# Four moves in a two-layer hybrid kernel: the last state-space outputs, the D scaling, one chunk of GpSimd's weighting, two slices of a down projection

## What is computed

```
xs, bm, cm = jnp.split(xbc, [SSM_D_INNER, SSM_D_INNER + SSM_GROUPS * SSM_STATE], axis=-1)
for d in range(2):
    v_ssm = (xs * dt[..., None]).reshape(b, L, SSM_GROUPS, SSM_RATIO, SSM_HEADDIM)
    y, s = chunked_decay_scan(fl(cm), fl(bm), fl(v_ssm), fl(la_ssm), s0)
    ssm_ys.append(fl(y).reshape(b, L, SSM_HEADS, SSM_HEADDIM) + d_skip[d][:, None] * xs)
y_ssm = (ssm_ys[0] + ssm_ys[1]).reshape(b, L, SSM_D_INNER)
y_ssm = rms_norm(y_ssm * jax.nn.silu(z)) * norm_gain
```

```
def conv_ffn(h, w_up, conv_w, conv_b, w_down):
    u = dwconv3(h @ w_up, conv_w, conv_b)
    a, val = jnp.split(u, 2, axis=-1)
    return (jax.nn.silu(a) * val) @ w_down
```

## Time and profile before

| | us |
|---|---|
| median of 3 runs | 1973.29 |
| lowest and highest | 1973.1, 1974.2 |
| the profiled execution's own time | 1970.14 |
| its span in the trace | 1968.4 |
| PE busy (share of the span) | 1896.4 (96%) |
| DVE busy | 1267.4 (64%) |
| ACT busy | 817.2 (42%) |
| POOL busy | 122.5 (6%) |

### The profile page before, as it was taken

How to read it: one execution, slowest core, us unless ns; L and a number is a source line. 1 busy time by engine, 2 the same in 40 slices (tenths; PEclk the granted TensorE clock), 3 DMA queues, 4 the chain that set the end, 5 groups by cost and what they waited for, 6 DMA issues and landing times.

```text
span 1968.4 us, 33247 instructions
## 1 busy us (share of the span) xinstructions
PE 1896.4 (96%) x13415; PEld 1800.2 (91%) x13415; DVE 1267.4 (64%) x2101; ACT 817.2 (42%) x1367; POOL 122.5 (6%) x106
## 2 busy tenths in 40 slices
PE   7999999999999999999999999899999999999999
PEld 4998789999988899999999989866698999999999
DVE  5555944666877877878978876656536553553553
ACT  4645732222435355234234344555525541441441
POOL 0011200000010000000000025411100000000000
PEclk9999999999999999999999999999999999999999
DMA  8221012444321323443433322100012222222222
GB/s 308 86 77 34 17 49 89 140 147 151 102 81 54 129 100 119 144 128 115 152 128 115 110 89 68 57 1 1 1 54 61 74 69 80 76 71 76 75 69 79
DMA packets 57065, 175.96 MB, mean 89 GB/s; under 512 B 7552, under 2 KB 9472, under 8 KB 56832
## 3 DMA queue, kind: packets, MB, share of 16 engines
q1 hardware_dynamic: 55152, 172.17, 27.1%
q10 hardware_dynamic: 1808, 2.36, 0.3%
HBM read 170.05 MB, written 4.46 MB: 89 GB/s over the span
## 4 chain that ended last, share of the span: by engine, by line
PE 84%; DVE 9%; ACT 4%; issue 2%; DMA 1%; SPq 1%; POOL 0%; ACTq 0%; DVEq 0%
PE ps L379 70%; PE ps L2103 2%; PE ps L2088 2%; DVE t_sb L772 1%; DVE h_lo L782 1%; PE ps L879 1%; DVE w_lo L368 1%; PE ps L2056 1%; DVE PT L2220 1%; PE ps L1294 1%; PE ps L2055 1%; ACT w_hi L360 1%; PE ps L1281 1%; PE ps L1305 1%; DMA x<-in_x 1%
## 5 line engine op out<-in xcount | busy, mean ns | idle before, releaser
L379 PE MATMUL ps<-h_hi,w_hi 128*128 128x320 f32 x2768 | 637.5, 311 | 7.8 <-DVE w_lo L368 2.9
L379 PE MATMUL ps<-h_lo,w_hi 128*128 128x320 f32 x2768 | 633.0, 310 | 9.0 <-DVE h_lo L782 7.8
L379 PE MATMUL ps<-h_hi,w_lo 128*128 128x320 f32 x2768 | 629.8, 308 | 0.0
L368 DVE TENSOR_TENSOR w_lo<-raw,w_hi 128x1024 fp32r<-128x1024 f32 (+1 forms) x218 | 267.2, 1226 | 452.6 <-ACT w_hi L360 452.3
L360 ACT ACTIVATE w_hi<-raw 128x1024 fp32r<-128x1024 f32 (+1 forms) x221 | 230.6, 1043 | 695.4 <-PE ps L379 695.2
L379 PEld LDWEIGHTS ps<-h_lo,w_hi 128*128 128x128 f32 x2768 | 461.4, 188 | 16.1 <-DVE h_lo L782 14.5
L379 PEld LDWEIGHTS ps<-h_hi,w_hi 128*128 128x128 f32 x2768 | 460.5, 188 | 15.1 <-issue 5.2
L379 PEld LDWEIGHTS ps<-h_hi,w_lo 128*128 128x128 f32 x2768 | 462.6, 188 | 0.0
L379 PE MATMUL ps<-hid_hi,w_hi 128*128 128x320 f32 x704 | 160.9, 309 | 4.4 <-DVE hid_lo L981 2.5
L379 PE MATMUL ps<-hid_hi,w_lo 128*128 128x320 f32 x704 | 160.2, 308 | 0.0
L379 PE MATMUL ps<-hid_lo,w_hi 128*128 128x320 f32 x704 | 160.2, 308 | 0.0
(11 more groups left out here) (285 smaller groups left out, 2014.7 us busy)
## 6 DMA issues: line engine op xcount, KB each, us to landing
raw<-in_ffn_up SPq DMA_DIRECT2D x88, 512.0 KB, 3.6
raw<-in_hyb_in SPq DMA_DIRECT2D x49, 512.0 KB, 3.8
mrawB<-in_w_modB SPq DMA_DIRECT2D x48, 512.0 KB, 4.2
mrawA<-in_w_modB SPq DMA_DIRECT2D x64, 256.0 KB, 2.8
raw<-in_ffn_down SPq DMA_DIRECT2D x32, 448.0 KB, 3.3
raw<-in_hyb_out SPq DMA_DIRECT2D x16, 512.0 KB, 4.2
raw<-in_ffn_down SPq DMA_DIRECT2D x16, 512.0 KB, 3.6
modw<-in_w_modA SPq DMA_DIRECT2D x12, 512.0 KB, 13.3
```

Source lines behind the costliest of these rows:

```text
L368: eng.tensor_tensor(w_lo[:, i % 2, 0:n], raw[:, b % RAW, 0:n], w_hi[:, i % 2, 0:n].bitcast(F32), SUB).then_inc(S("w_lo"), 1)
L379: last = pe.matmul(pj(f)[:, hh, :], w[:, i % 2, k * 128:(k + 1) * 128], v[:, k, hh * HALF:(hh + 1) * HALF], start=(k == 0 and n == 0), sto ...
```

## The change

There are four edits.

1. In `pe_ssd` the last iteration no longer issues the outputs of pass 7. `pe_z` writes its first unit out slice by slice and issues them, all five chunks, between the slices 4 and 5 of that unit.
2. In `act_ssd` the D scaling stands behind the copy of the final state, ahead of the exponentials of load 3; before it stood between the exponentials of loads 1 and 2.
3. In `pool_ssd` the weighting for direction 0 covers chunks 0 to 3, and no longer chunk 4.
4. In `pe_first` the three down stages of layer 0 take four slices of unit 1 ahead of the last slice of unit 0, and no longer two. Layer 1 keeps two.

```diff
-                steps = [(0, k) for k in range(K - 1)] + [(1, 0), (1, 1), (0, K - 1)] + [(1, k) for k in range(2, K)]
+                m = 4 if units[0][0].name[:3] == "dn0" else 2
+                steps = [(0, k) for k in range(K - 1)] + [(1, k) for k in range(m)] + [(0, K - 1)] + [(1, k) for k in range(m, K)]
...
-                if p:
+                if 0 < p < PAIRS:
                     pe_out(pe, p - 1, (0, 1, 2))
...
-                if p:
+                if 0 < p < PAIRS:
                     pe_out(pe, p - 1, (3, 4))
...
                         act_decay(act, p, i)
-                        if i == 1:
-                            act_skip(act, p)
                     act.wait_ge(S("ssd_kv"), p + 1)
...
                                    ACT.Copy).then_inc(S("ssd_so"), 1)
+                    act_skip(act, p)
                     act_decay(act, p, 3)
...
                 for d in range(2):
-                    scaled(xw[:, p % 2, d, :, :], wdt[:, :, d, 2 * p:2 * p + 2].unsqueeze(3).to_broadcast([128, NCH, 2, 64]))
+                    n = NCH - 1 + d
+                    scaled(xw[:, p % 2, d, 0:n, :], wdt[:, 0:n, d, 2 * p:2 * p + 2].unsqueeze(3).to_broadcast([128, n, 2, 64]), n)
...
-            for r in range(8):
-                pe_unit(pe, stages["z"], r, 0, H)
+            s = stages["z"]
+            pe_begin(pe, s, 0)
+            for k in range(KT):
+                if k == 5:
+                    pe_out(pe, PAIRS - 1, (0, 1, 2))
+                    pe_out(pe, PAIRS - 1, (3, 4))
+                last = pe_tile(pe, s, 0, k, s.u0, s.f0, H)
+            last.then_inc(S("pe_unit"), 1)
+            for r in range(1, 8):
+                pe_unit(pe, s, r, 0, H)
```

More of the change, by code:

```diff
@@ L1421, in pool_ssd, with scaled @@
                 xh = xs_chunks(p).rearrange("p c (h v) -> p c h v", h=2)
-                def scaled(out, by):
-                    pool.tensor_tensor(out.rearrange("p c (h v) -> p c h v", h=2), xh, by, MUL).then_inc(S("ssd_v"), 1)
+                def scaled(out, by, n):
+                    pool.tensor_tensor(out.rearrange("p c (h v) -> p c h v", h=2), xh[:, 0:n, :, :], by, MUL).then_inc(S("ssd_v"), 1)
                 if p >= 2:
```

## The result

| | before | changed kernel |
|---|---|---|
| median of the runs, us | 1974.2 (5 runs) | 1964.82 (5 runs) |
| lowest and highest | 1973.1, 1974.83 | 1963.59, 1964.95 |
| the profiled execution's own time | 1970.14 | 1964.69 |
| its span | 1968.4 | 1962.9 |

The ratio is 0.995, with a 95% interval of 0.9937 to 0.9964: the kernel became faster by 9.4 us. I had forecast 1966.9 and at the best 1964.9, so the direction was right and the time lies just outside the range. The table already shows what has to be explained. The two profiled executions differ by 5.45 us, less than the 6.4 of my sum. The two medians differ by 9.4.

The account below looks back on a forecast made before the run. PE was taken to bound the kernel, busy 1896.4 of 1968.4 us, with gaps and slow-clock stretches to win. Terms 4.9 + 0.9 + 0.6 + 0 = 6.4 us off the median 1973.29 gave 1966.9, range 1964.9 to 1969.9.

Parts of the forecast that it names:

- the range: Whole kernel: 8 in 10 for 1964.9 to 1969.9 us, the forecast's bounds plus some 0.6 scatter of medians either side.
- my sum: Whole kernel: the four edits' gains, 4.9 + 0.9 + 0.6 + 0 = 6.4 us; this forecast had chance 0.62.
- the gain by z's end: End of z: everything behind it is released by PE or loaded ahead, so the 5.5 us gained by then stays.
- The step that failed: Whole kernel: the 6.4 us found on the profiled execution of 1970.14 was taken off the median of 1973.29, giving 1966.9.
- Edit 1: End of passes: PE's idle 3.80 us goes and the outputs run at full clock; 4.9 us less, bounds 4.2 and 5.2.
- Edit 2: Pass 0: exponentials of load 2 and the state's copy come 0.8 earlier; 0.9 us less, bounds 0.5 and 1.1.
- the clock of pass 0 stays up too: Rival, pass 0: with the second idle stretch gone PE may stay at 2.4 GHz; gain 7.0, 1966.3 us, chance 0.10.
- Edit 3: Passes 2 to 4: shorter GpSimd instruction delays DVE less, 0.2 us three times; 0.6 us less, bounds 0 and 0.75.
- Edit 4: Layer 0 down stages: dn01 wins 0.7 us, dn02 0, dn00 loses 0.7; together 0, bounds 0.7 either way.
- a fall lands elsewhere: Clock: a fall's place differs from run to run, so the pass 0 clock rival and the forecast would both occur.

Follow-up runs that it names:

- skip_only: Kernel before with only the D scaling moved behind the final state's copy: 1971.54 us, ratio 0.9987.
- mix: fill_after with D scaling moved back, four slices only in dn01, 6 unread matmuls added in pass 0, 9 in dn02: 1963.86 us, ratio 0.9951.
- fill_after: Changed kernel plus matmuls nobody reads in PE's waits, 14 in pass 0 and 12 ahead of dn02's unit 2: 1963.89 us, ratio 0.9952.
- rest_no_z: Changed kernel with the outputs of pass 7 taken back out of z's first unit: 1968.77 us, ratio 0.9972.
- fill_before: Kernel before, order kept, plus matmuls nobody reads in four PE waits (two in pass 0, last outputs, dn01): 1968.72 us, ratio 0.9973.

## Why the prediction was off

**The sum was nearly right for the profile it was made on.** At the places of the edits matched matmuls give 7.0 (6.80 up to z's second unit and 0.16 in the down stages), against 6.4. That 1970.14 - 6.4 = 1963.7 also comes within 1.0 of the changed kernel's profiled execution, 1964.69, is luck in part: 3.1 lost in retention and 0.99 at the start stand against some 2.8 won in attention, all outside the edits. One slip in the working: it calls the gain by z's end 5.5, and its own terms are 4.9 + 0.9 + 0.6 = 6.4 there. The forecast used the 6.4.

**The step that failed is the one behind the sum**: "The median of the runs shown is 3.15 above it; the sum off the median". It takes what one profile shows for what the median gains, with the falls of the clock where that profile had them: a gain by the clock at z, where it had one, and nothing by it in pass 0, dn01 and dn02. The runs show that this doesn't hold. The same program lost 7.9 us and 12.9 us to the lower clock in two executions, filling four waits won 5.2 us on an unchanged path, and edits 2 to 4 won 5.5 (3.0 to 7.9) where the sum has 1.5.

As a sum, the 9.38 are 5.45 between the two profiled executions, plus 1974.2 - 1970.14 = 4.06 from the profile of before to its median, less 0.13 from the profile of the changed kernel to its own. I had 6.4 for the first and nothing for the difference of the other two, which is 3.9. But this 3.9 is not the edits' own: chance in retention, in attention and at the start is in it. By place, in the means of the traces, I come to an estimate of 7.4: 5.05 at z, 1.5 from pass 0 to the outputs of pass 2, 0.44 for edit 3 in passes 3 and 4, 0.16 on the path of the down stages, and by the clock 1.0 won in dn01 and 0.8 lost in dn02. That is 1.0 more than the forecast. The other 2.0 of the 9.4 stay open; the result's own interval is 7.1 to 12.4 us, so part of them can be scatter.

- **Edit 1 was right**: 5.05 in the trace against 4.9, 5.1 alone in the ratio. The outputs begin behind the fifth slice without a wait for DVE (idle 0.19 of PE's weight loads, none of its matmuls), took 2.33 at a clock of 1.00 (2.26 forecast), and the wait for `w_lo` is 0.18 (0.3 forecast). Some 1.5 of the 5.05 is the clock: it is the term of z in the table, in all six traces that kept the unfilled idle time and in none of the six with the outputs inside z.
- **Edit 2: the mechanism holds only where the clock falls, and the size was too small.** I took it for 0.9 on the path. From the first decay load to the outputs of pass 2 it is 37.06 to 38.61 us, in the mean 37.8, in the five traces with the old order unfilled, against 35.89 to 37.11, in the mean 36.3, in the five with the new order: 1.5 won, which lies in the interval of the run alone (1.0 to 4.3). Most of this is there at an equal loss in pass 0, 1.6 in the profile of before and 1.7 in `skip_only` (the first decay load and the outputs of pass 2, first before, then `skip_only`):

```profile
174.88 0.50 PE L1250 MATMUL ps<-neg_r,ident_r 128*128 128x512 f32 x1 [0.46 <-ACT t_sb L845]
212.10 0.29 PE L1305 MATMUL ps<-u_sb,xsy 128*64 128x128 f32 x1 [1.43 <-issue]
...
176.90 0.50 PE L1250 MATMUL ps<-neg_r,ident_r 128*128 128x512 f32 x1 [0.46 <-ACT t_sb L845]
212.92 0.29 PE L1305 MATMUL ps<-u_sb,xsy 128*64 128x128 f32 x1 [1.43 <-issue]
```

  That is 37.22 against 36.02, 1.2 less. PE at the lower clock is what holds the chain there: in `skip_only` DVE's pair is through 14.95 us behind the first decay load, and PE gets to the outputs of pass 0 only at 15.52 (16.72 before). So the 0.8 by which load 4 comes earlier arrives in full, and a part of the fall now lies ahead of load 4. Where the clock stays up, GpSimd meets DVE's pair, and the same move costs 0.6 (`mix` against `fill_after`). The loss in pass 0 is 1.5 to 3.1, in the mean 2.4, in the old order and 0 to 3.1, in the mean 1.6, in the new one. That the move makes the fall shorter is not shown by so few traces. My rival "the clock of pass 0 stays up too" came out once in five (`rest_no_z`), and there the stretch of 36.34 is no shorter than with a fall.
- **Edit 3 was right in mechanism**: GpSimd's pair takes 2.72 instead of 2.93 beside DVE, and PE's wait ahead of the outputs of passes 2 to 4 fell from 1.43 to 1.21, three times 0.22, 0.66 against 0.6. Alone it can't be measured in the time.
- **Edit 4 was right on the path and left out the clock.** By matched matmuls of the two traces dn00 lost 0.60, dn01 won 0.76 and dn02 is unchanged (forecast: 0.7, 0.7 and 0). But the wait of 2.50 in dn01 was followed by a fall in three of five traces, and the two waits of 0.73 in none of seven. The 2.06 in dn02 was followed by one in two of four, the 1.71 in none of seven. With 1.6 for a fall that is some 1.0 won in dn01 and 0.8 lost in dn02.
- **The range** took the scatter of medians as 0.6. Single runs of the kernel before lie between 1967.75 and 1978.14. A range drawn from one profile should have held at least a fall or two, 1.6 us each, on either side. The measured 1964.82 missed its lower end by 0.1.

The Trainium skill (TensorE: Matmul & The Clock Gate, "What's actually happening") says that the monitor of activity runs free of the kernel's start, and gives this as the reason why the point at which the clock changes varies from run to run. By that rule equal waits would be followed by a fall in some executions only, and the traces agree: three of five behind the 2.50 of dn01. My reading of it in the prediction, that a fall lands elsewhere, goes further than the traces: behind the first decay load all but one of the falls (at 1210 in `fill_before`) stand in the six places of the table.

## What to carry to other kernels

An idle time of PE costs more than its length where the clock falls behind it: list the long idle times (here a fall came behind 2.06 us and more, not behind 1.71), and shorter ones close together, and count for each a part of a fall as well, and try a few matmuls that nobody reads in them before reordering anything, since here they brought 5.2 us in an unchanged order. Take the falls out of a profile before you compare or extrapolate it, or compare the same instructions of both traces place by place, and never carry the distance between a profile and a median over to another kernel. Work moved behind a copy to free one engine stands ahead of something else: look at what the next two instructions of that engine feed.

## What the runs showed of the hardware

- **The clock falls behind waits much shorter than I had thought to matter**, and behind some of them only in a part of the executions: behind 3.80 us in six of six traces, behind 2.34 with a second one of 0.91 to 1.21 after it in five of five, behind 2.34 with at most 0.38 after it in four of five, behind 2.50 in three of five, behind 2.06 in two of four, behind 1.71 in none of seven and behind a pair of 0.73 in dn01 in none of seven. One fall costs 1.4 to 1.7 us of PE's work.
- **A long stretch at the lower clock in retention** costs 4.8 to 5.1 us in nine of the thirteen traces. In the changed kernel PE is idle 0.41, 0.50 and then 1.06 us between 557 and 562, and the clock is low until 572 although PE is busy from 562 on:

```profile
557.85 1.38 PE L1620 MATMUL ps<-qkT 64*128 64x128 f32 x10 [0.41 <-DVE x L895]
560.14 0.49 PE L1653 MATMUL ps<-vTM,PTr 128*128 128x128 f32 x2 [0.50 <-DVE PTr L1772]
561.69 0.58 PE L1653 MATMUL ps<-vTM,PTr 128*128 128x128 f32 x1 [1.06 <-DVE Sr L1762]
```

The same place as stretches of 1 us, for PE alone (length, busy time, granted clock, DMA share, GB/s):

```profile
562.00:563.00 1.00, 1.00 (x6) 0.50 0.00 0
...
571.00:572.00 1.00, 1.00 (x12) 0.62 0.00 0
572.00:573.00 1.00, 1.00 (x22) 1.00 0.08 16
```

In the profile of before the same waits (0.40, 0.50 and 1.06) were followed by a loss of 1.7 only. Why it lasts so long in most executions was not tried. It is the largest loss in eleven of the thirteen traces, with the change and without it.
- **GpSimd beside DVE**: in `fill_after` GpSimd's first instruction began 0.75 us into DVE's pair, and the pair took 0.86 more (2.34 against 1.48 in `fill_before`, where GpSimd began 0.16 behind the pair's end). To move work by a microsecond was enough to make the two meet.
